# Order of work at two stage borders and of the tail norms in a fused attention, DeltaNet and MLP block

## The reference

```python
h = rms_norm(x, pre_mix_norm)
proj = h @ w_in                      # 1024 x 3600, columns by head group
fq, fk, fv, ff, gq, gk, gv, gb, ga, gz = jnp.split(proj, split_at, axis=-1)
log_f = log_sigmoid(ff + fox_f_bias)
fox_o = rms_norm(forgetting_attention(fq, fk, fv, log_f), fox_out_norm)
qkv = silu(causal_depthwise_conv(concat([gq, gk, gv]), gdn_conv_w))
beta = sigmoid(gb)
g = -exp(gdn_a_log) * softplus(ga + gdn_dt_bias)
gdn_o = gated_delta_chunked(l2norm(cq), l2norm(ck), cv, g, beta)
gdn_o = rms_norm(gdn_o, gdn_out_norm) * silu(gz)
mixed = concatenate([fox_o, gdn_o]) @ w_out
x = x + rms_norm(mixed, post_mix_norm)
h = rms_norm(x, pre_mlp_norm)
y = square(relu(h @ w_up)) @ w_down
x = x + rms_norm(y, post_mlp_norm)
```

## Time and profile before

| | us |
|---|---|
| median of 3 runs | 1574.5 (1572.85 to 1576.81) |
| the profiled execution's own time | 1574.49 |
| its span in the trace | 1572.7 |
| PE busy | 1422.9 (90%) |
| DVE busy | 1017.9 (65%) |
| ACT busy | 645.8 (41%) |
| POOL busy | 674.6 (43%) |
| mean granted TensorE clock | 0.957 of full |

### The profile page before, as it was taken

How to read it: one execution, slowest core, us unless ns; L and a number is a source line. 1 busy time by engine, 2 the same in 40 slices (tenths; PEclk the granted TensorE clock), 3 DMA queues, 4 the chain that set the end, 5 groups by cost and what they waited for, 6 DMA issues and landing times.

```text
span 1572.7 us, 20750 instructions
## 1 busy us (share of the span) xinstructions
PE 1422.9 (90%) x7389; PEld 1189.9 (76%) x7389; DVE 1017.9 (65%) x1604; ACT 645.8 (41%) x1278; POOL 674.6 (43%) x570
## 2 busy tenths in 40 slices
PE   4899999966987988889779979999999998999997
PEld 3678888846977887878768867888888786688885
DVE  5857777735566666666534588776666569844557
ACT  5544334414453453544423362333333243445443
POOL 3523333206446284472520156666666349631001
PEclk9899999987999999999879999999999999999999
DMA  6133333235222112110322223444444795333533
GB/s 195 41 109 107 108 107 107 81 103 165 68 73 63 41 59 73 32 41 1 94 80 81 87 75 121 147 154 148 150 151 148 272 334 183 87 100 95 203 98 141
DMA packets 135325, 177.88 MB, mean 113 GB/s; under 512 B 10492, under 2 KB 82732, under 8 KB 135224
## 3 DMA queue, kind: packets, MB, share of 16 engines
q1 hardware_dynamic: 135224, 176.56, 35.0%
HBM read 124.05 MB, written 52.48 MB: 112 GB/s over the span
## 4 chain that ended last, share of the span: by engine, by line
PE 72%; DVE 14%; POOL 4%; issue 4%; DMA 2%; ACT 2%; SPq 1%; DVEq 0%; ACTq 0%; POOLq 0%
PE ps L2867 6%; PE ps L2869 6%; PE ps L2868 6%; PE ps L2627 6%; PE ps L2568 6%; PE ps L2570 6%; PE ps L2569 6%; PE ps L2880 4%; PE ps L2882 4%; PE ps L2881 4%; PE ps L2752 3%; DVE db_lo L2183 3%; DVE da_lo L2181 3%; PE ps L2821 2%; PE ps L2819 2%
## 5 line engine op out<-in xcount | busy, mean ns | idle before, releaser
L2880 PE MATMUL ps<-db_hi,da_hi 128*128 128x512 f32 x448 | 177.7, 397 | 10.8 <-DVE db_lo L2183 10.7
L2881 PE MATMUL ps<-db_lo,da_hi 128*128 128x512 f32 x448 | 174.6, 390 | 0.0
L2882 PE MATMUL ps<-db_hi,da_lo 128*128 128x512 f32 x448 | 174.5, 390 | 0.0
L2181 DVE TENSOR_TENSOR da_lo<-a_raw,da_hi 128x512 fp32r<-128x512 f32 x112 | 103.4, 923 | 100.7 <-ACT da_hi L1654 100.7
L1654 ACT ACTIVATE da_hi<-a_raw 128x512 fp32r<-128x512 f32 x112 | 70.7, 631 | 173.0 <-PE ps L2882 152.5
L2867 PE MATMUL ps<-bt_hi,ring_hi 128*128 128x512 f32 x320 | 127.2, 397 | 5.4 <-DVE ring_lo L2103 5.2
L2869 PE MATMUL ps<-bt_hi,ring_lo 128*128 128x512 f32 x320 | 127.9, 400 | 0.0
L2868 PE MATMUL ps<-bt_lo,ring_hi 128*128 128x512 f32 x320 | 127.0, 397 | 0.0
L2568 PE MATMUL ps<-i_bt_hi,i_ring_hi 128*128 128x512 f32 x280 | 112.7, 403 | 8.4 <-DVE i_u L1834 4.8
L2438 POOL TENSOR_TENSOR o_rs<-o_ms,halves 128x1 f32<-128x1 f32 x24 | 16.5, 687 | 230.8 <-DVE o_ms L2206 111.4
L2880 PEld LDWEIGHTS ps<-db_hi,da_hi 128*128 128x128 f32 x448 | 84.0, 188 | 39.0 <-DVE db_lo L2183 22.4
(11 more groups left out here) (352 smaller groups left out, 3776.2 us busy)
## 6 DMA issues: line engine op xcount, KB each, us to landing
a_raw<-act_dram SPq DMA_DIRECT2D x112, 256.0 KB, 2.6
act_dram<-s_act SPq DMA_DIRECT2D x64, 256.0 KB, 2.0
wd<-in_w_down_dram SPq DMA_DIRECT2D x15, 1024.0 KB, 7.3
act_dram<-c SPq DMA_DIRECT2D x48, 256.0 KB, 5.0
w_top<-in_w_up_dram SPq DMA_DIRECT2D x18, 512.0 KB, 4.5
w_bot<-in_w_up_dram SPq DMA_DIRECT2D x16, 512.0 KB, 5.7
i_top<-in_w_in_dram SPq DMA_DIRECT2D x14, 512.0 KB, 4.0
i_bot<-in_w_in_dram SPq DMA_DIRECT2D x14, 512.0 KB, 5.4
```

What stands on the lines that cost most here:

```text
L2181: nc.vector.tensor_tensor(da_lo[s][:, :], a_raw[n % 4][:, :], da_hi[s][:, :].bitcast(F32), ALU.subtract).then_inc(d_lo_ready, 1)
L2880: nc.tensor.matmul(acc, da_hi[s][:, cols], db_hi[s][:, :], start=start, stop=False, skip_group_check=True)
L2881: nc.tensor.matmul(acc, da_hi[s][:, cols], db_lo[s][:, :], start=False, stop=False, skip_group_check=True)
L2882: return nc.tensor.matmul(acc, da_lo[s][:, cols], db_hi[s][:, :], start=False, stop=stop, skip_group_check=True)
```

## The change

Three places are reordered, and no arithmetic is added or left out.

1. **Entry and gate chain.** `x_out` of tile 4 goes ahead of `i_hi(0,2)` and `p1_out(0)` on ACT. On DVE `i_lo(0,2)` goes behind `x_n` of tile 6, and `gate_w_lo` goes behind `x_out` of tile 6 and `i_lo(1,2)`. The four ACT steps of the gates go behind the turns 0 to 2 of pair 0, the five DVE steps behind turns 3 and 4 of pair 0 and turns 0 to 2 of pair 1, and the Exp for beta one place behind the scan. `gate_y` moves to other memory, under `i_p1[2]`, so that `p1_out(2)` waits for the gates and `c_out(1,5)` no longer does. The two stores to `gate_dram` go one pair later.
2. **Border to the head stage.** The stores of pairs 12 and 13 go from ahead of all loads of head 0 to behind `load_g_row(0)` and behind `load_c("v", 0)`.
3. **Tail norms.** But for the last head, the attention norm is planned at +8 and +12 instead of +4, one half of the tokens each; the DeltaNet norm at +8 instead of +6. In the last head only the order within the norm changes: half 0 is finished before half 1 is begun.

```diff
-            at("dve", t + 6.0, "tail_norm", tail)
+            at("dve", t + (6.0 if last else 8.0), "tail_norm", tail, c // 4)
...
-            at("dve", v + 4.0, "tail_norm", tail)
+            for half in range(2):
+                at("dve", v + (4.0 if n == 2 * GDN_HEADS - 1 else 8.0 + 4.0 * half), "tail_norm", tail, half)
...
-        gate_y = placed("gate_y", 106752, [P, SEQ])
+        gate_y = placed("gate_y", 131328, [P, SEQ])
...
-            for f in range(NPAIR + 1):
+            for f in range(NPAIR):
...
-                if f == 1:
+                if f == 2:
                     sp.wait_ge(gate_dve, 5)
...
+            sp.wait_ge(stored, 32)
...
-            sp.wait_ge(stored, 32)
             sp.wait_ge(i_lo_ready, len(IN_SPLIT_ORDER))
             sp.wait_ge(i_s_ready, 4 * NPAIR)
             load_c("k", 0)
...
             load_g_row(0)
+            store_pair(NPAIR - 2)
             load_c("v", 0)
+            store_pair(NPAIR - 1)
             load_c("z", 0)
             load_fox(1)
...
                 elif f == 2:
-                    act.wait_ge(x_turned, NT)
+                    act.wait_ge(gate_dve, 4)
+                    act.wait_ge(gate_act, 5)
...
+                if t >= 2:
+                    x_out(t - 2)
                 if t == 6:
                     i_hi(0, 2)
                     p1_out(0)
-                if t >= 2:
-                    x_out(t - 2)
...
+            def gates(n):
+                if n == 0:
...
+                    nc.scalar.activation(gate_u[:, :], gate_y[:, :], ACT.Abs).then_inc(gate_act, 1)
+                elif n == 1:
...
+                    nc.scalar.activation(gate_u[:, :], gate_u[:, :], ACT.Exp, scale=-1.0).then_inc(gate_act, 1)
+                elif n == 2:
...
+                    nc.scalar.activation(gate_u[:, :], gate_u[:, :], ACT.Ln, bias=1.0).then_inc(gate_act, 1)
...
                     for g, j in in_splits_after(f, i):
                         i_hi(g, j)
-                    if f == 1 and n == 0:
+                    if f == 0:
+                        gates(n)
+                    if f == 1 and n == 2:
                         act.wait_ge(gate_dve, 4)
...
                 if t == 5:
                     i_lo(1, 1)
+                if t == 6:
+                    i_lo(0, 2)
+            x_out(NT - 2)
+            i_lo(1, 2)
             dve.wait_ge(gate_w_hi_ready, 1)
             nc.vector.tensor_tensor(gate_w_lo[:, :, :], gate_w[:, :, :], gate_w_hi[:, :, :].bitcast(F32), ALU.subtract).then_inc(gate_w_lo_ready, 1)
-            i_lo(0, 2)
-            x_out(NT - 2)
-            i_lo(1, 2)
...
-                    elif f == 1:
-                        dve.wait_ge(gate_dve, 5)
-                        dve.wait_ge(gate_act, 5)
...
-                    if f == 0 and n == 1:
-                        gates()
                     for g, j in in_splits_after(f, i):
                         i_lo(g, j)
+                    if f == 0 and n >= 3:
+                        gates(n - 3)
+                    if f == 1 and n < 3:
+                        gates(n + 2)
...
-            def norm(tail):
+            def norm(tail, half):
                 dve.wait_ge(tail_power, TAIL[tail])
                 if tail[0] == "fox":
                     h = tail[1]
-                    for half in range(2):
...
```

More of the change, by code:

```diff
@@ L254 @@
 TAIL = numbered(TAILS)
-TAIL_NORMS = [item[1] for item in ORDER["dve"] if item[0] == "tail_norm"]
-NORMS = [(t, half) for t in TAIL_NORMS for half in range(2 if t[0] == "fox" else 1)]
+NORMS = [item[1:] for item in ORDER["dve"] if item[0] == "tail_norm"]
 NORM = numbered(NORMS)
@@ L663, in heads_over @@
             eng.wait_ge(mixed_ready, len(NORMS))
[L665 to L668, removed]
         proj_dram = nc.dram_tensor("proj_dram", (GDN_HEADS, len(KIND_ROW), P, SEQ), F32, kind="Internal").ap()
@@ L1040, in load_w_out @@
                     sp.wait_ge(scan_done, (GDN_HEADS - 1) * NCHUNK)
-                    sp.wait_ge(mixed_ready, NORM[(("gdn", GDN_HEADS - 2, 1), 0)])
+                    sp.wait_ge(mixed_ready, NORM[(("gdn", GDN_HEADS - 2, 1), 1)])
                 if c >= 7:
@@ L1341, in _ @@
             i_hi(0, 3)
[L1342 to L1348, removed]
+            def gates(n):
+                if n == 0:
+                    act.wait_ge(gate_read, 2)
+                    nc.scalar.activation(gate_u[:, :], gate_y[:, :], ACT.Abs).then_inc(gate_act, 1)
+                elif n == 1:
+                    act.wait_ge(gate_act, 1)
+                    nc.scalar.activation(gate_u[:, :], gate_u[:, :], ACT.Exp, scale=-1.0).then_inc(gate_act, 1)
+                elif n == 2:
+                    nc.scalar.activation(row_a[:, 1:2], row_a[:, 0:1], ACT.Exp).then_inc(gate_act, 1)
+                    act.wait_ge(gate_act, 2)
+                    nc.scalar.activation(gate_u[:, :], gate_u[:, :], ACT.Ln, bias=1.0).then_inc(gate_act, 1)
             def gates_out(half):
@@ L1424, in read @@
                 if what == "z" and g == 0 and p >= 2:
-                    act.wait_ge(mixed_ready, NORM[(("gdn", p - 2, 1), 0)])
+                    act.wait_ge(mixed_ready, NORM[(("gdn", p - 2, 1), 1)])
                 if what == "fv" and g == 0 and p >= 2:
@@ new lines, in gates @@
+            def gates(n):
+                if n == 0:
+                    dve.wait_ge(gate_act, 4)
+                    dve.wait_ge(gate_read, 2)
+                    nc.vector.scalar_tensor_tensor(out=gate_y[log_rows, :], in0=gate_y[log_rows, :], scalar=0.0, in1=gate_u[log_rows, :],
+                                                   op0=ALU.min, op1=ALU.subtract, reverse1=True).then_inc(gate_dve, 1)
+                elif n == 1:
+                    nc.vector.scalar_tensor_tensor(out=gate_y[g_rows, :], in0=gate_y[g_rows, :], scalar=0.0, in1=gate_u[g_rows, :],
+                                                   op0=ALU.max, op1=ALU.add).then_inc(gate_dve, 1)
+                elif n == 2:
+                    dve.wait_ge(gate_dve, 2)
+                    nc.vector.tensor_scalar(gate_y[g_rows, :], gate_y[g_rows, :], row_a[g_rows, 1:2], -1.0, ALU.mult, ALU.mult).then_inc(gate_dve, 1)
+                elif n == 3:
+                    dve.wait_ge(gate_dve, 3)
+                    dve.wait_ge(keep_loaded, 16)
+                    nc.vector.tensor_tensor_scan(gate_rows[:, :], keep[:, :], gate_y[:, :], 0.0, ALU.mult, ALU.add).then_inc(gate_dve, 1)
+                else:
+                    dve.wait_ge(gate_dve, 4)
+                    by_chunk = gate_rows[g_rows, :].rearrange("p (n c) -> p n c", c=CHUNK)
+                    nc.vector.tensor_tensor(gate_rows[r_rows, :].rearrange("p (n c) -> p n c", c=CHUNK),
+                                            by_chunk[:, :, CHUNK - 1:CHUNK].to_broadcast([GDN_HEADS, NCHUNK, CHUNK]), by_chunk,
+                                            ALU.subtract).then_inc(gate_dve, 1)
@@ L2051, in _ @@
                 else:
-                    norm(n)
+                    norm(n, item[2])
             heads_over(dve)
```

35 lines of the change are left out of this document (8 added, 27 removed).

## The result

| | before | after |
|---|---|---|
| median, us | 1574.2 (4 runs, 1572.85 to 1576.81) | 1539.7 (4 runs, 1536.31 to 1543.34) |
| ratio | | 0.9771, interval 0.9756 to 0.9786 |
| the profiled execution's own time | 1574.49 | 1541.79 |
| its span | 1572.7 | 1540.0 |
| mean granted TensorE clock | 0.957 | 0.971 |

The kernel is 36 us faster by the ratio, 34.5 by the medians. The forecast was 1536, its range 1525 to 1550. The four runs of after lie 7 us apart by themselves, the five of the repeat 1.5 us.

What follows compares the result with a forecast made beforehand. PE was taken as the bound, with time won only where it idles or runs at half clock. 3.0 + 8.4 + 13 + 15 + 0.6 - 1.3 = 38.7 us; 1574.5 - 38.7 = 1536, range 1525 to 1550.

Steps and rivals of the forecast that it cites:

- 1a, entry: Entry: the wait before block product (0,2) goes, a new one opens between the gate products' halves; gain 3.0 us.
- 1b, gate chain: Pairs 0 and 1: spread gate steps shorten the wait before (0,4) and remove that before (0,3); gain 8.4 us.
- 2, border: Border to the head stage: with loads ahead of the last stores, `k_hi(0)` starts 13.0 us earlier; gain 13 us.
- 3, norms: Head stage: norms later and in pieces remove three PE waits and the slow clock behind them; gain 15 us.
- the last head: Last head's norm: half 0 is ready one step sooner and PE starts its transposes on it; gain 0.6 us.
- the cleared state: Last scan's start: the DeltaNet norm of head 2 stands right ahead of the clearing PE waits for; -1.3 us.
- 1 us for each of six pieces: Head stage: cost taken off the norms' gain, with 2 us more in head 1: 23.7 - 8 = 15.7.
- (a): Head stage rival: GpSimd holds up the norm's pieces and they reach PE, norms give only 6.6: 1544; chance 0.18.
- (b): Border rival: stores late behind the loads or `k_hi(0)` waits longer, 7 instead of 13: 1542; chance 0.09.
- (c): Pair 1 rival: gates make DVE late to `c_out(1,5)`, and no gain at the entry: 1543; chance 0.08.
- (d): Head stage rival: many short waits keep PE at 1.2 GHz, slower than 1574.5; chance 0.02.
- (e): Border rival: the change does not do what it says, the first load waits for the last weight split; chance 0.01.

Runs made afterwards that it cites:

- the repeat: The kernel after, unchanged, measured a second time: 1536.6 us, ratio 0.9758 to the kernel before.
- e5_whole: Kernel after, but the attention norm of heads 0 to 2 not cut, both halves together at +8: 1535.8 us, ratio 0.9765.
- e11_early_pieces: Kernel after, but the two pieces of the attention norm of heads 0 to 2 at +4 and +8 instead of +8 and +12: 1543.4 us, ratio 0.9802.
- e10_gdn_six: Kernel after, but the second half of the DeltaNet norm of head 2 back at +6: 1536.35 us, ratio 0.9757.
- e4_norms: Kernel before with only the norms' change, later and in pieces: ratio 0.9908, 14.5 us.

## Why the prediction was right

The sum was 38.7 us; 34.5 to 38.5 were measured by medians. Step by step:

- **1a, entry, 3.0 forecast.** 3.9 and 3.3 us in the two executions of after, 3.6 alone. The wait was moved into the gate products, as told, but it is 2.65 us and not 4, since the last `bt_lo` is ready at 48.6 and not 49.5, and PE came to it at 46.0 and not 45.6.
- **1b, gate chain, 8.4 forecast.** 6.5, 7.8 and, alone, 7.9. The wait before (0,4) shrank by 1.7 us, the text's lower figure, because `i_lo(1,6)` took 1.38 us beside GpSimd (0.69 before), and 3.16 was left instead of 2.8. "The one before (0,4) I keep at 1.4" is the step that varies: the same wait was followed by 8 or by 14 slow matmuls, 1.2 us apart. The claims of no wait before (0,3) and none in pair 1 held.
- **2, border, 13 forecast.** 10.5 and 11.2, alone 11.1. The mechanism was as told, with one term too small and one left out. `k_hi(0)` came 10.2 us behind the end of `w_in`, not 8.5 (0.5 of that because the last store was issued 4.2 us behind it and not 3.7, 1.0 because it took longer to land): "only `load_c("v")` is put between them" was costed at nothing, but the transfers share the DMA engines. In after's picture of DMA from 326 to 345 (slices of 0.475 us) the slices from the first store to the last landing are full but for one or two; what they move is three stores and the loads of v and z, five times 0.5 MB:

```profile
DMA  0000000000009999986999999993000000000979
GB/s 0 0 0 0 0 0 0 0 0 0 0 0 405 414 285 276 198 224 216 423 423 414 423 423 414 431 405 147 0 0 0 0 0 0 0 0 0 129 293 328
```

  The load of v is 0.5 MB; at 423 GB/s it pushes the last store back by 1.2 us (an estimate), and that store took 5.9 us to land, where the earlier trace rows had 4.9. The Trainium skill (SBUF — State Buffer, A bandwidth-pool intuition that's wrong (but worth ruling out)) gives the path between the DMA engines and SBUF 436 GB/s; the 423 are 3% under it. The scale of k made part of it good: the power of k took 2.06 us beside a DVE step (1.02 before), but GpSimd was free for it sooner, and from `k_hi(0)` to the scale it was 4.6 us, where the prediction had 5.5 and the kernel before 5.4. So the scale came 11.7 us sooner against the end of `w_in`, and PE's lead just behind it had grown by 11.7 (11.6 in the repeat). What was left out is the low clock behind the wait: eight us later the growth was 10.5 (11.2).
- **3, norms, 15 (14.3 with the last head and the cleared state) forecast.** 12.0 and 15.8, alone 14.5 by ratio. The total is near, in part by luck. The place that the 15 us stood for, the first three heads, gave 11.5, 11.9 and, alone, 11.1 us; 1.6 us that no term had came ahead of the first norm, and from the last scan to `w_out` it was -1.1, 2.3 and, alone, 5.4 us against a forecast of -0.7. And half of the reason was wrong. "It is cut in two pieces with items between, which PE needs" claimed a gain that isn't there: not cut, the norm gives the same (e5_whole), and cut but early it loses 4 to 7 us (e11_early_pieces). What wins in the first three heads is the later place. With it goes the time that DVE stood idle for the power (6.6 us before and in e11_early_pieces, none in after); how much of the gain is that, and how much the norm's own steps no longer standing ahead of what PE waits for, no run tells apart. The DeltaNet norms at +8 and the order in the last head were never tried without the rest, so the 5.4 us of the last stage have no cause shown but that less time passes at the low clock. "1 us for each of six pieces" stood for costs that are real but of another kind: GpSimd's queue behind the power, 4.65 us of wait in head 0, where the prediction promised at most 2.
- **The cleared state, -1.3.** The wait is 1.2 to 1.3 us longer, as told. It is worth 0.7 at the end (e10_gdn_six against the repeat), and nothing that the time shows.
- **Rivals.** (a), the norm's steps held up by GpSimd: the first scale took 2.20 us and the weight 1.63 against 0.68 and 0.69 for the second piece, as the rule of the Trainium skill that the prediction names (SBUF — State Buffer, Who interferes with whom) has it: GpSimd was at work beside the first piece and idle beside the second. But PE was not held by them, and part 3 gave its 12 to 16, not 6.6. (b), the stores late behind the loads: true by 1.7 us, not by 6. (c), (d) and (e) did not come.

What stays open: why the same wait is followed by a shorter stretch at 1.2 GHz in one execution and a longer one in another. It was measured, not explained. The same holds for the last stage of the head work, which took 66.4, 63.4, 62.9 and 58.5 us in before, after, its repeat and e4_norms. Why the three first parts win 1.6 us ahead of the first norm was read only as less low clock there; it wasn't tried by itself.

## What to carry to other kernels

When an engine stands idle in order for a short result of another engine, put the consumer later rather than cut it into pieces, and then look at what is queued behind the producer, since that is the next wait. At a border between stages, ask which byte of a buffer ties the first write to the last store: an overlap of 108 bytes a partition was worth 5 us here. Before two traces of one kernel and another are compared to the microsecond, look at a second execution of the same kernel.

## What was not expected of the hardware

The same kernel, with its waits of over 3 us up to `w_out` the same to within 0.1 us, had 90 and 80 us at the low clock in two executions, worth some 5 of the 5.6 us between their spans. A wait of 3.16 us was followed by 8 us at a mean clock of 0.57 in one and 0.79 in another kernel with the same instructions there. What the low clock costs at a wait is thus a range (1.2 us wide for the wait of 3 us, 2.9 for the stretch before the last scan), and by the 5.6 us between two executions of one kernel a sum of many such terms is good to some 3 us either way at best.
